# Down weights fetched as two transfers of 2 MB with 16 KB in one piece per partition, activations turned in fours of columns

## The reference, cut to what matters

```
def expert_block(args):
    xb, e = args                                   # 128 rows of tokens, one expert
    gu = xb @ w_gu[e] + b_gu[e]                    # w_gu[e]: 1024 x 2048, 8 MB
    gate, up = jnp.split(gu, 2, axis=-1)
    gate = jnp.minimum(gate, 7.0); up = jnp.clip(up, -7.0, 7.0)
    glu = gate * jax.nn.sigmoid(1.702 * gate)
    return ((up + 1.0) * glu) @ w_down[e] + b_down[e]   # w_down[e]: 1024 x 1024, 4 MB
```

## Time and profile before

| | us |
|---|---|
| median of three executions | 1465.04 |
| lowest, highest | 1462.0, 1465.07 |
| the profiled execution, time | 1465.49 |
| the profiled execution, span | 1463.6 |
| PE, DVE, ACT, POOL busy | 1328.7, 839.1, 727.7, 361.0 |
| loads of w_gu: 256 of 1024 KB, median to landing | 9.7 |
| loads of w_down: 128 of 1024 KB, median to landing | 10.8 |

### The profile page before, as it was taken

The page is one execution under the profiler, slowest core; times in us unless marked ns, Lnnn a source line. Parts: engine busy times, 40 slices in busy tenths (PEclk is TensorE's granted clock), DMA queues, the critical chain, the costliest instruction groups (busy, mean ns, idle before and its releaser), DMA issues.

```text
span 1463.6 us, 17803 instructions
## 1 busy us (share of the span) xinstructions
PE 1328.7 (91%) x6418; PEld 866.9 (59%) x6423; DVE 839.1 (57%) x947; ACT 727.7 (50%) x940; POOL 361.0 (25%) x318
## 2 busy tenths in 40 slices
PE   4999999999999897998979898989899897998986
PEld 1657885558757374775554675737477465756432
DVE  0576775446947273775463774727378446758234
ACT  3542325546736354665372763636466536637222
POOL 2000020112133232321423332323233141413220
PEclk9999999998999999999999999999999999999998
DMA  9656530055989999999999999999999999999996
GB/s 343 201 166 230 204 131 15 9 195 183 341 329 403 400 371 403 381 396 383 383 392 386 383 390 390 390 385 364 399 370 402 384 373 383 392 383 381 383 392 217
DMA packets 95129, 475.90 MB, mean 325 GB/s; under 512 B 23687, under 2 KB 33903, under 8 KB 42817
## 3 DMA queue, kind: packets, MB, share of 16 engines
q1 hardware_dynamic: 82656, 451.39, 78.4%
q0 software_dynamic: 12304, 23.22, 5.9%
q10 hardware_dynamic: 80, 0.13, 0.0%
HBM read 468.16 MB, written 23.09 MB: 336 GB/s over the span
## 4 chain that ended last, share of the span: by engine, by line
PE 69%; DMA 14%; ACT 9%; DVE 4%; SPq 2%; issue 2%; DVEq 0%; ACTq 0%
DMA ring<-in_w_down 13%; PE bank L1727 9%; PE bank L1730 9%; PE bank L1734 9%; PE bank L1776 6%; PE bank L1761 4%; PE bank L1511 4%; ACT e_hi L906 3%; PE bank L1323 3%; PE bank L1806 3%; PE bank L1325 3%; PE bank L1324 3%; ACT area L909 3%; PE bank L1798 3%; PE bank L1799 2%; DVE e_lo L1984 2%
## 5 line engine op out<-in xcount | busy, mean ns | idle before, releaser
L1984 DVE TENSOR_TENSOR e_lo<-ring,e_hi 128x2048 fp32r<-128x2048 f32 x216 | 485.0, 2287 | 269.4 <-ACT e_hi L906 269.2
L906 ACT ACTIVATE e_hi<-ring 128x2048 fp32r<-128x2048 f32 x216 | 409.6, 1919 | 317.7 <-DMA ring<-in_w_down 254.7
L1761 PE MATMUL bank<-ring,area 128*64 128x512 f32 x896 | 204.0, 602 | 37.8 <-DMA ring<-in_w_gu 37.8
L1727 PE MATMUL bank<-e_hi,x_hi 128*128 128x512 f32 x576 | 227.2, 394 | 0.0
L1730 PE MATMUL bank<-e_hi,x_lo 128*128 128x512 f32 x576 | 224.7, 390 | 0.0
L837 POOL COPY future<-routes 128x1 int32 (+1 forms) x31 | 113.9, 3674 | 395.6 <-DVE area L2320 274.8
L1798 PE MATMUL bank<-e_hi,act_hi 128*128 128x512 f32 x288 | 121.3, 421 | 50.1 <-ACT e_hi L906 50.0
L1761 PEld LDWEIGHTS bank<-ring,area 128*64 128x64 f32 x896 | 60.3, 137 | 171.6 <-issue 101.2
L1734 PE MATMUL bank<-e_lo,x_hi 128*128 128x512 f32 x576 | 154.2, 390 | 0.0
L1727 PEld LDWEIGHTS bank<-e_hi,x_hi 128*128 128x128 f32 x576 | 108.2, 188 | 26.2 <-issue 4.1
L1734 PEld LDWEIGHTS bank<-e_lo,x_hi 128*128 128x128 f32 x576 | 108.2, 188 | 22.7
(11 more groups left out here) (296 smaller groups left out, 1734.3 us busy)
## 6 DMA issues: line engine op xcount, KB each, us to landing
ring<-in_w_gu SPq DMA_DIRECT2D x256, 1024.0 KB, 9.7
ring<-in_w_down SPq DMA_DIRECT2D x128, 1024.0 KB, 10.8
ring<-in_ada_w SPq DMA_DIRECT2D x24, 1024.0 KB, 9.2
ring<-in_w_in SPq DMA_DIRECT2D x9, 1024.0 KB, 7.9
ring<-in_w_o SPq DMA_DIRECT2D x4, 1024.0 KB, 7.7
xs<-in_x SPq DMA_DIRECT2D x4, 512.0 KB, 5.2
ring<-in_w_in SPq DMA_DIRECT2D x8, 256.0 KB, 5.3
xn_rows<-area POOLq DMA_DIRECT2D x4, 512.0 KB, 5.1
```

What stands on the lines that cost most here:

```text
L906: return nc.scalar.activation(dst, src, ACT.Copy, scale=scale)
L1727: pe.matmul(bank[b][:], x_hi[:, c, :], hi, start=False, stop=False)
L1761: mm = pe.matmul(bank[g // 2][half, :], xgT[:, c, 0:NARROW], w[:, 512 * g:512 * g + 512], start=False, stop=(c == GU - 1))
L1984: tt(e_lo[c % PARTS][:], raw(period.raw_slot(c)), e_hi[:, c % PARTS, :].bitcast(F32), ALU.subtract).then_inc(lo_ready, 1)
```

## The change

Down weights are fetched by `down_pair` instead of `down_chunk`: two transfers of 2 MB for an expert instead of four of 1 MB. A transfer brings 512 rows of 4 KB; a partition gets four neighbouring rows, 16 KB in one piece in device memory and in two neighbouring slots of the ring. It waits until both slots are free. Two new semaphores tell of the landing, one for each pair, and all readers of either slot wait for it. The partition p now holds rows 4p to 4p+3 of a half of the down weights, so the transposes take every fourth column of the activations instead of every second.

```
-                return raw_in[s], self.i * 32 + 16 * (c // SLOTS + (1 if s >= 4 else 0))
+                i, opening = self.i, 2 if s >= 4 else 1
+                if isinstance(i, int) and i <= E:
+                    if i == E:
+                        return down_in[2 + c // 2], 16
+                    if c >= GU:
+                        return down_in[(c - GU) // 2], i * 16
+                    return raw_in[s], 16 * (opening + (i - 1) * (2 if s < 2 else 1) + c // SLOTS + 1)
...
-            def down_chunk(period, c, q, e):
+            def down_pair(period, c, pair, e):
                 s = period.raw_slot(c)
-                src = w_down[e, 2 * q * P:(2 * q + 2) * P, :].rearrange("(p k) n -> p k n", k=2)
-                sp.dma_start(raw(s).rearrange("p (k n) -> p k n", k=2), src).then_inc(raw_in[s], 16)
+                if isinstance(period.i, int):
+                    raw_free(period, c)
+                raw_free(period, c + 1)
+                src = w_down[e, 4 * pair * P:(4 * pair + 4) * P, :].rearrange("(p k) n -> p k n", k=4)
+                dst = ring[:, s * SLOT:(s + 2) * SLOT].rearrange("p (k n) -> p k n", k=4)
+                sp.dma_start(dst, src).then_inc(down_in[pair if c >= GU else 2 + pair], 16)
...
-                for q in range(DN):
-                    raw_free(period, GU + q)
-                    down_chunk(period, GU + q, q, e_before)
+                for pair in range(DN // 2):
+                    down_pair(period, GU + 2 * pair, pair, e_before)
...
             def closing(i, e_before):
                 period = Later(i)
+                if i == E:
+                    for pair in range(DN // 2):
+                        down_pair(period, 2 * pair, pair, e_before)
+                    return
...
             def turn_narrow(half):
-                pairs = act[:, 0:512].rearrange("p (q f k) -> p q k f", q=2, k=2)
+                fours = act[:, 0:512].rearrange("p (f k) -> p k f", k=4)
                 for k in range(2):
-                    mm = pe.transpose(bank[6 + half][:, k * P:(k + 1) * P], pairs[:, half, k, :], ident[:])
+                    mm = pe.transpose(bank[6 + half][:, k * P:(k + 1) * P], fours[:, 2 * half + k, :], ident[:])
...
-                pairs = act.rearrange("p (q f k) -> p q k f", q=DN, k=2)
+                fours = act.rearrange("p (q f k) -> p q k f", q=2, k=4)
                 for q in range(4):
-                    mm = pe.transpose(bank[6 + half][:, q * P:(q + 1) * P], pairs[:, 2 * half + q // 2, q % 2, :],
-                                      ident[:])
+                    mm = pe.transpose(bank[6 + half][:, q * P:(q + 1) * P], fours[:, half, q, :], ident[:])
```

More of the change, by code:

```diff
@@ L345, in build @@
         raw_in = [sem(f"raw_in{i}") for i in range(SLOTS)]
+        down_in = [sem(f"down_in{i}") for i in range(DN)]
         hi_ready, lo_ready, chunk_used = sem("hi_ready"), sem("lo_ready"), sem("chunk_used")
@@ L473, in landed @@
                 s = self.raw_slot(c)
-                return raw_in[s], 16 * ((self.n0 + c + 4) // SLOTS + (1 if s >= 4 else 0))
+                before = (2 if s >= 4 else 1) + (E - 1) * (2 if s < 2 else 1) if self.i else 0
+                return raw_in[s], 16 * (before + c // SLOTS + 1)
         class Later:
@@ L488, in landed @@
                 s = c % SLOTS
-                return raw_in[s], self.i * 32 + 16 * (c // SLOTS + (1 if s >= 4 else 0))
+                i, opening = self.i, 2 if s >= 4 else 1
[5 more added lines that the diff above has]
+                    return raw_in[s], 16 * (opening + (i - 1) * (2 if s < 2 else 1) + c // SLOTS + 1)
+                if c >= GU:
+                    return down_in[(c - GU) // 2], i * 16 - 16
+                return raw_in[s], i * (32 if s < 2 else 16) + 16 * (2 * opening - (4 if s < 2 else 2) + c // SLOTS + 1)
         def rows_of(t):
@@ L632, in down_chunks @@
                 period = Later(i)
-                for q in range(DN):
-                    raw_free(period, GU + q)
-                    down_chunk(period, GU + q, q, e_before)
+                for pair in range(DN // 2):
+                    down_pair(period, GU + 2 * pair, pair, e_before)
             def closing(i, e_before):
                 period = Later(i)
+                if i == E:
+                    for pair in range(DN // 2):
+                        down_pair(period, 2 * pair, pair, e_before)
+                    return
                 for q in range(DN):
                     raw_free(period, q)
-                    down_chunk(period, q, q, e_before)
+                    fours = w_down[e_before, 4 * (q // 2) * P:4 * (q // 2 + 1) * P, :]
+                    sp.dma_start(raw(q).rearrange("p (k n) -> p k n", k=2),
+                                 fours.rearrange("(p k) n -> p k n", k=4)[:, 2 * (q % 2):2 * (q % 2) + 2, :]
+                                 ).then_inc(raw_in[q], 16)
             sp.wait_ge(act_taken, A_RV + 2 * T)
```

## The result

| | before | changed |
|---|---|---|
| median of six executions each | 1463.04 us | 1486.15 us |
| lowest, highest | 1460.12, 1465.07 | 1478.47, 1488.45 |
| the profiled execution's span | 1463.6 us | 1486.7 us |

The ratio is 1.0152, with a 95% interval from 1.0132 to 1.0172: the change makes the kernel 1.5% slower. The forecast was 1.3%, in a range of 1466 to 1499 us. The two profiled executions took 1465.49 and 1488.45 us, each some 2.4 us more than its median, so their difference is that of the medians, 23 us.

What follows compares the result with a forecast made beforehand. The prediction took nearly full transfer engines, in a ring through ACT and PE, as the bound. Its terms, 16.8 + 1.0 + 1.9 - 3 + 2 = 18.7 us, gave 1483.5 us, 1.3% slower, range 1466 to 1499.

Steps and rivals of the forecast that it cites:

- What bounds the kernel: Expert part: full transfer engines; ring from chunk 9's landing through compute, a freed slot and eight loads to the next landing.
- Part 1: Narrow periods: ACT's first two high parts wait for one landing; what follows starts 1.91 us later, 24.8 us if unabsorbed.
- Part 2: Down-load issue: waiting for two slots costs 0 by itself; with the 1.91 us delay, transfer engines idle in wide periods.
- The term of 1.4 us a ring: Idle transfer engines, 1.4 us for each of 12 narrow periods that a wide one follows: 16.8 us, bounds 0 and 1.91.
- The thirteenth ring: Last of 13 narrow periods, followed by a narrow one with loads longer in the queue: +1.0 us, between 0 and 1.9.
- part 3: End of the experts: the last two chunks land together, so both are multiplied behind the last load: +1.9 us.
- Part 4: Weight queue q1: fewer, longer packets, 512 fewer per engine at 6 ns each: -3 us.
- Part 5: PE's transposes of every fourth column instead of every second: +2 us, up to 20 us if weight loads are not hidden.
- Absorption: Rival for the rings: loads far enough ahead absorb the delay, other terms cancel, 1465 +- 3 us; chance 0.12.
- the faster rival: Weight queue: longer packets get twice the turn against POOL's gathers, the pair lands sooner, 1450 us; chance 0.07.
- Slow long packets: Rival for the weight transfers: 16 KB packets take 883 ns against 668 for twice 8 KB, 1575 us; chance 0.03.
- The upper case: Rival: ACT's delay unabsorbed, transposes at their upper end, and the clock: 24.8 + 1.9 + 20, 1512 us; chance 0.06.

Runs made afterwards that it cites:

- land_first_only: Kernel before; only in 13 narrow periods behind a wide one, ACT's high part of down chunk 8 also waits for chunk 9's landing: 1492.4 us, 1.0201.
- land_others: Kernel before; ACT's high parts wait for both landings of a pair everywhere except the first pair in narrow periods: 1464.9 us, 1.0013.
- fours_split: Changed kernel, still waiting for two slots, but each pair fetched as two 1 MB loads with a semaphore for each half: 1471.3 us, 1.0050.
- issue_pair: Kernel before, four 1 MB loads with a landing each; only SP waits for both slots of a pair before issuing its first load: 1471.1 us, 1.0051.
- both_pair: Kernel before, four 1 MB loads; SP waits for two slots, ACT and PE's narrow matmuls wait for both landings of a pair: 1485.5 us, 1.0155.
- fours_by_slot: Changed kernel's rows and transposes in fours, but each pair as two 1 MB loads, each waiting for its own slot alone: 1461.8 us, 1.0004.
- before_act_first: Kernel before; in narrow periods behind a wide one ACT makes activation and next tokens before the high parts of chunks 8 and 9: 1479.1 us, 1.0107.
- before_first_filled: Kernel before with ACT's activation and tokens ahead of the high parts, plus 18 PE matmuls of zeros before down in narrow periods behind wide ones: 1482.0 us, 1.0146.
- after_filled: Changed kernel, ACT's order unchanged, plus 14 PE matmuls of zeros before down in narrow periods behind a wide one: 1500.4 us, 1.0239.
- run 14: Not a run's number: words from "in a run 14 us slower", said of after_filled, 14 us slower than the changed kernel: 1500.4 us.

## Why the prediction was right, point by point

**What bounds the kernel** stood: a ring of landing, ACT, PE, a freed slot and eight loads at full rate, 13 times, with the engines full.

**Part 1** stood as a mechanism and in its size. Predicted was 1.91 us more between the landing and the activation; the trace has 3.73 - 1.94 = 1.79, and 1.8 in each of the 13 periods. The place is shown by land_first_only against land_others, and the changed kernel without the joint landing (fours_split) loses 8 us instead of 23.

**Part 2** had the right sign and was too small in one respect. It said that the wait for two slots costs 0 by itself and matters only with part 1; issue_pair costs 8 us, 0.3 to 0.7%. The sum went by one period, had 0.85 us of reserve there and took the queue for one stream. Its times were good: with the landing at 503.47 before and 502.88 after, the pair was to be issued 24.95 us behind it and went at 527.77, which is 24.89. But the landing came later than the sum had it: 530.7 + 4.96 = 535.7, or 535.0 with the issue 0.65 us earlier, and the trace has it 8.9 us behind the issue, at 536.65. Two periods on the pair issued at 599.32 takes 7.7 us (the least of all pairs is 7.6), against 2.3 + 4.96 = 7.3 reckoned. It was issued 1.33 us before the last load ahead of it landed (600.65), and in the three half microseconds from 600.5 on the DMA share is 0.74, 0.60 and 0.49. So a queue that holds about one load when the pair is issued runs dry. The term of 1.4 us a ring measured 2.0 (24.4 over 12). It was made a minimum of ACT's 1.91 and the idle time of the transfers, with part of ACT's delay absorbed; nothing was absorbed in the mean. This term, 16.8 us, is the one that was mis-sized, by 7.6, and what it left out is the wait for two slots: 8 us by issue_pair, whose 12 rings are 6.1 us longer.

**The thirteenth ring**, +1.0, and **part 3**, +1.9, were wrong in sum. From the 13th narrow activation to the last instruction the changed kernel is 1.3 us shorter. At the end of the experts both chunks of the last pair do come behind its landing:

```profile
1462.74 3.30 PE bank L1796 x8
...
1466.30 1.89 PE bank L1796 x8
...
1470.42 5.42 PE bank L1932 x12
```

The same place of the kernel before:

```profile
1443.80 2.03 PE bank L1901 x12
1445.83 6.97 PE bank L1912 x12
```

The two chunks take 5.5 us instead of 1.96, more than the 3.8 that were named, since the first runs at a granted clock of 0.57. It is given back behind. The 12 matmuls that add the last rows take 5.42 us at a granted clock of 1.00, where the kernel before took 6.97 at 0.77, after PE had been idle for 1.94 us; and the 2.03 us of bias sums (L1901) that stood in the chain there now run beside DVE's work. From the last landing to the end are 24.0 us, before 23.7. The other 1.6 us of the difference lie ahead of that landing. None of this was in the sum.

**Part 4**, -3, can't be told from 0 in the time: both_pair with packets of 8 KB and the changed kernel with 16 KB are 0.6 us apart, with some 2.5 to 3 us of uncertainty each. q1 took 0.781 x 16 x 1486.7 us / 73,440 = 253 ns a packet of 6,146 bytes, 24.3 bytes a ns, before 24.6: no gain by length is to be seen there. In the records of the single packets the median of 8 KB is 309 ns and that of 16 KB is 611, 7 ns less than two of 8 KB, close to the 6 ns that were taken. **Part 5**, +2, can't be told from 0 either: fours_by_slot has -1.6 to +2.9 us, and the weight load of the transposes is as long as before (209 ns in the earlier trace rows):

```profile
L1722 PEld LDWEIGHTS bank<-ident,area x144: 195/209/219, 382.6 to 1390.4; 128*128 128x128 f32 x144
```

The Trainium skill (SBUF — State Buffer, section Door 1: The DMA port swizzle) would have every fourth fp32 pay more; in this weight load it pays nothing more than every second. And the prediction read the step of two wrongly beside it: with two hits in a line the rule has it at full rate, so the 209 ns against 140 speak against the rule here and not for it. That the step makes the difference is not shown either, since the weight loads of `x_hi` in L1727, of contiguous columns, take 188 ns. The Trainium skill (DMA: Bandwidth & Descriptors, section Anatomy of one DMA) has about 2 us of fixed cost for a transfer that POOL (GpSimd) issues, while SP issues these; carried over to them, as the prediction did, that makes an estimate of up to 128 us for the 64 transfers. None of it is seen here.

**The sum.** Predicted were 16.8 for the 12 rings and 1.9 for the rest (1.0 + 1.9 - 3 + 2), together 18.7; measured in the two profiled executions are 24.4 and -1.3, together 23.1. The term of the rings was 7.6 too small, and 3.2 too much in the others hid nearly half of that. The forecast in per cent is better than its terms, and that much of it is luck.

**The rivals.** Absorption is out by the rings' 24.4 us; the four rings with two wide periods, where loads were to be far ahead, lost 2.3 us each and the others 1.9. For the faster rival the pair would have had to land in under 11 us; in the first ring it took 13.51. Slow long packets are out by both_pair, and a packet of 16 KB on q1 took 656 ns in the mean, not 883. The upper case did not come: its 24.8 us for part 1 is near what the rings lost, but by issue_pair and fours_split 8 us of that are part 2, and part 5 had nothing of its 20 us.

## What to carry to other kernels

Joining two loads joins their landings and their waits for space, and both have a price where the reader works chunk by chunk: the work that lay beside the second load moves behind it. Look up in the chain what stands right behind a landing, and in whose program order: here one line of ACT's order, 13 times, was two thirds of the loss. To tell the parts of such a change apart, put its waits alone into the old kernel; with two waits and no other edit it gave 1.0155 against 1.0152.

## What the runs showed of the hardware that was not expected

A higher granted clock need not save time: work of zeros raised the mean of a run from 0.96 to 0.99 and left its time as it was (before_act_first, before_first_filled), and in another run (after_filled) it moved the low level from a place beside ACT's work into the chain, in a run 14 us slower. Yet land_others has the low level at the same place of its chain in 12 of 13 periods and is only 2 to 3 us from the kernel before. The length of the pieces, 8 or 16 KB to a partition, made no difference to the time that could be told from noise (1485.5 and 1486.15 us), and 7 ns to the median of a packet. Two waits that cost 31 and 8 us alone cost 23 together; why is open.
